# Relative-position rows of four heads in one product, stored once and repeated by a DMA within device memory

## The reference

```python
def _group_bias(rel_bias, g, dil):
    qi = np.arange(ATT_BLOCK)[:, None]            # ATT_BLOCK = 128
    kj = np.arange(2 * ATT_BLOCK)[None, :]
    dist = np.maximum(qi + ATT_BLOCK - kj, 0) * dil
    bucket = _t5_causal_bucket(dist)
    tab = rel_bias[:, g * ATT_HEADS_PER_GROUP:(g + 1) * ATT_HEADS_PER_GROUP]
    return jnp.transpose(tab[bucket], (2, 0, 1)).astype(jnp.float32)
...
    logits = jnp.einsum('zhnqd,zhnkd->zhnqk', qs, kb).astype(jnp.float32) * (hd ** -0.5)
    logits = jnp.where(valid, logits + bias[:, None], NEG_INF)
```

## Time and profile before

| | |
|---|---|
| median of 3 runs | 1987.79 us (1986.08, 1987.95, 1987.79) |
| the profiled execution | 1989.3 us; its span from first to last instruction 1987.5 us |
| PE busy | 1939.8 us, 98% of the span |
| DVE, ACT, POOL busy | 959.8, 779.9, 62.5 us |
| mean granted clock of PE | 0.989 of full |
| share of PE in the chain that ended last | 95% |

### The profile page before, as it was taken

How to read it: one execution, slowest core, us unless ns; L and a number is a source line. 1 busy time by engine, 2 the same in 40 slices (tenths; PEclk the granted TensorE clock), 3 DMA queues, 4 the chain that set the end, 5 groups by cost and what they waited for, 6 DMA issues and landing times.

```text
span 1987.5 us, 30907 instructions
## 1 busy us (share of the span) xinstructions
PE 1939.8 (98%) x12878; PEld 1607.1 (81%) x12878; DVE 959.8 (48%) x1515; ACT 779.9 (39%) x1221; POOL 62.5 (3%) x123
## 2 busy tenths in 40 slices
PE   7999988999999999999999999999999999999996
PEld 5887788868788888888699988788888888888885
DVE  6557634465444344446643226544344554344436
ACT  5354543362443133335543252332422442233343
POOL 0000000000320000000001100000000000000000
PEclk9999999999899999999999999999999999999998
DMA  4222100024432222222322222222233332222222
GB/s 168 97 82 78 64 24 4 14 64 138 128 114 96 96 97 102 98 96 95 106 86 86 86 75 97 84 75 78 82 120 117 108 100 96 96 96 95 96 85 85
DMA packets 51969, 178.99 MB, mean 90 GB/s; under 512 B 7103, under 2 KB 7615, under 8 KB 51840
## 3 DMA queue, kind: packets, MB, share of 16 engines
q1 hardware_dynamic: 45184, 161.50, 24.3%
q0 software_dynamic: 5968, 14.48, 2.4%
q10 hardware_dynamic: 688, 1.11, 0.2%
HBM read 168.41 MB, written 6.55 MB: 88 GB/s over the span
## 4 chain that ended last, share of the span: by engine, by line
PE 95%; DVE 2%; issue 1%; ACT 1%; DMA 0%; ACTq 0%; DVEq 0%
PE bank L659 94%; PE bank L841 0%; DVE ring_lo L1849 0%; PE bank L723 0%; DMA x<-in_xT 0%; DVE work_r L1905 0%; ACT work L1336 0%; PE bank L1266 0%; DVE nr L1863 0%; PE bank L813 0%; DVE hf L1885 0%; DVE work_r L1854 0%; DVE bias L2077 0%; DVE work L2297 0%; ACT ring_hi L1336 0%
## 5 line engine op out<-in xcount | busy, mean ns | idle before, releaser
L659 PE MATMUL bank<-work_r,ring_hi 128*128 128x512 f32 x2592 | 810.5, 392 | 14.5 <-DVE ring_lo L1849 13.2
L1849 DVE TENSOR_TENSOR ring_lo<-ring,ring_hi 128x1024 fp32r<-128x1024 f32 x302 | 367.8, 1224 | 626.1 <-ACT ring_hi L1336 626.0
L659 PEld LDWEIGHTS bank<-work_r,ring_hi 128*128 128x128 f32 x2592 | 488.2, 188 | 119.1 <-DVE ring_lo L1849 13.7
L1336 ACT ACTIVATE ring_hi<-ring 128x1024 fp32r<-128x1024 f32 x302 | 318.5, 1057 | 537.3 <-DMA ring<-in_stream 535.1
L659 PE MATMUL bank<-work_r,ring_lo 128*128 128x512 f32 x1296 | 506.8, 391 | 0.0
L659 PE MATMUL bank<-h_hi,ring_hi 128*128 128x512 f32 x864 | 341.5, 395 | 0.0
L659 PE MATMUL bank<-h_hi,ring_lo 128*128 128x512 f32 x864 | 337.7, 391 | 0.0
L659 PEld LDWEIGHTS bank<-work_r,ring_lo 128*128 128x128 f32 x1296 | 244.8, 189 | 50.8 <-issue 0.7
L659 PE MATMUL bank<-h_lo,ring_hi 128*128 128x512 f32 x864 | 212.3, 389 | 0.0
L659 PEld LDWEIGHTS bank<-h_hi,ring_hi 128*128 128x128 f32 x864 | 163.1, 189 | 40.7 <-issue 6.4
L659 PEld LDWEIGHTS bank<-h_hi,ring_lo 128*128 128x128 f32 x864 | 163.1, 189 | 34.7 <-issue 1.2
(11 more groups left out here) (226 smaller groups left out, 1590.1 us busy)
## 6 DMA issues: line engine op xcount, KB each, us to landing
ring<-in_stream SPq DMA_DIRECT2D x302, 512.0 KB, 3.3
scratch<-work POOLq DMA_DIRECT2D x12, 192.0 KB, 2.5
x<-in_xT POOLq DMA_DIRECT2D x8, 256.0 KB, 2.9
spill<-x POOLq DMA_DIRECT2D x1, 2048.0 KB, 9.2
work<-x POOLq DMA_DIRECT2D x32, 64.0 KB, 2.1
x<-spill POOLq DMA_DIRECT2D x8, 256.0 KB, 3.0
outT<-hf SPq DMA_DIRECT2D x8, 256.0 KB, 2.1
x<-in_xT ACTq DMA_DIRECT2D x2, 512.0 KB, 8.4
```

The costliest lines, as they stand in the source:

```text
L659: ins = pe.matmul(out, lhsT, rhs, start=start, stop=stop, skip_group_check=True)
L1336: return nc.scalar.activation(out, in_, func, **kw)
L1849: v.tensor_tensor(ring_lo[:, n % RING, :, :], ring[:, n % RING, :, :], ring_hi[:, n % RING, :, :], ALU.subtract).then_inc(sem("split_lo"), 1)
```

## The change

Three `rel` jobs take the place of 12: job g multiplies the whole table (33x12) by the constant matrix of group g, so that row c of its bank is head c's row. ACT copies 12 rows. POOL stores the four rows of the group once each, waits for the three stores, and then three DMAs within device memory copy each row 127 times (group 0) or 39 times (groups 1 and 2) behind it; POOL waits for them before the same 48 skewed reads. The waits of ACT on the stores go; DVE waits for the three row stores instead.

```diff
--- before.py
+++ after.py
@@ -234,7 +234,7 @@
     first = 1 if blk == 1 else 5
     j = [("wo", blk, m) for m in range(DT)]
     if blk == 1:
-        j += [("rel", c) for c in range(12)]
+        j += [("rel", g) for g in range(3)]
     for half in range(2):
         j += [("f1", blk, half, i) for i in range(FF_H)]
         if half == 0:
@@ -599,13 +599,17 @@
 
             pool.dma_start(g2_sb[0:16, :], wa2).then_inc(sem("wa2_in"), 16)
 
-            for c in range(12):
-                pool.wait_ge(*is_drained("rel", c))
-                pool.dma_start(scratch[c, 0:P * RELW].rearrange("(p n) -> p n", n=RELW),
-                               work[:, 40 + c % 4, 0:RELW]).then_inc(sem(f"rel_out{c % 4}"), 16)
+            for g in range(3):
+                pool.wait_ge(*is_drained("rel", g))
+                pool.dma_start(scratch[4 * g:4 * g + 4, 0:RELW], work[4 * g:4 * g + 4, 40 + g, 0:RELW]).then_inc(sem("rel_rows"), 16)
+            pool.wait_ge(sem("rel_rows"), 16 * 3)
+            for g in range(3):
+                copies = (P if g == 0 else 40) - 1
+                pool.dma_start(scratch[4 * g:4 * g + 4, RELW:RELW + copies * RELW].rearrange("c (p n) -> c p n", n=RELW),
+                               scratch[4 * g:4 * g + 4, 0:RELW].unsqueeze(1).broadcast_to([4, copies, RELW])).then_inc(sem("rel_out"), 16)
+            pool.wait_ge(sem("rel_out"), 16 * 3)
             for c in range(12):
                 g, hh = divmod(c, 4)
-                pool.wait_ge(sem(f"rel_out{c % 4}"), 16 * (c // 4 + 1))
                 skew = scratch[c, P - 1:P - 1 + P * (RELW - 1)].rearrange("(p n) -> p n", n=RELW - 1)
                 for z in range(TT):
                     r = slice(32 * z, 32 * z + 32)
@@ -1090,11 +1094,10 @@
                 project(("pb", m), plain(*ob) if m else arriving("ob_hi", "ob_lo", *ob), 4, 4)
                 done_with(1)
 
-            def rel(c):
-
-                out = take("rel", c)
-                single(("rel", c), [(out[:, 0:RELW], tab[0:33, c:c + 1].broadcast_to([33, P]),
-                                     work[0:33, 32 + c // 4, 0:RELW], True, True)])
+            def rel(g):
+
+                out = take("rel", g)
+                single(("rel", g), [(out[0:12, 0:RELW], tab[0:33, 0:12], work[0:33, 32 + g, 0:RELW], True, True)])
 
             def tail(blk):
                 n0 = 1 if blk == 1 else 5
@@ -1106,8 +1109,8 @@
                 if blk == 1:
                     pe.wait_ge(sem("relc_in"), 16)
                     pe.wait_ge(sem("tab_in"), 16)
-                    for c in range(12):
-                        rel(c)
+                    for g in range(3):
+                        rel(g)
                 for half in range(2):
                     if half == 0:
                         normed_together([("f1", blk, 0, i) for i in range(TOGETHER)], n0)
@@ -1608,12 +1611,10 @@
                 act.wait_ge(sem("merged1"), m + 1)
                 high_part(R(MERGED_HI + m), W(MERGED + m), "merged_hi1")
 
-            def copy_rel(c):
-                split_hi(blocks_to("rel", c))
-                act.wait_ge(*computed("rel", c))
-                if c >= 4:
-                    act.wait_ge(sem(f"rel_out{c % 4}"), 16 * (c // 4))
-                f(work[:, 40 + c % 4, 0:RELW], bank(("rel", c))[:, 0:RELW], ACT.Copy).then_inc(bank_drained[nth("rel", c)], 1)
+            def copy_rel(g):
+                split_hi(blocks_to("rel", g))
+                act.wait_ge(*computed("rel", g))
+                f(work[0:12, 40 + g, 0:RELW], bank(("rel", g))[0:12, 0:RELW], ACT.Copy).then_inc(bank_drained[nth("rel", g)], 1)
 
             def tail(blk):
                 n0 = 1 if blk == 1 else 5
@@ -1623,8 +1624,8 @@
                     high(n0, m)
                     square(n0, m)
                 if blk == 1:
-                    for c in range(12):
-                        copy_rel(c)
+                    for g in range(3):
+                        copy_rel(g)
 
                 act.wait_ge(sem(f"l{n0}"), DT)
                 act.wait_ge(sem("sq_added"), added(n0) + DT - 1)
@@ -1763,9 +1764,6 @@
             inverse_roots(lambda n: W(ROOT_G + n), [("gn", n) for n in range(4)], 256, 0, "root_g")
             gla_gates(2, 8)
 
-            for c in range(8, 12):
-                act.wait_ge(sem(f"rel_out{c % 4}"), 16 * (c // 4 + 1))
-
             def probs2(i, h, t):
                 near, far = reach(t)
                 n = near + 2 * far
@@ -2272,8 +2270,7 @@
                         scale_of(n0)
                     elif blk == 1:
 
-                        for c in range(4):
-                            dve.wait_ge(sem(f"rel_out{c}"), 48)
+                        dve.wait_ge(sem("rel_rows"), 16 * 3)
                     for m in range(DT):
                         split_lo(blocks_to("f2", blk, half, m))
                         dve.wait_ge(*computed("f2", blk, half, m))
```

## The result

The changed kernel takes 1977.24 us (median of 5 runs, 1975.02 to 1978.5), the kernel before 1987.61 us beside it (5 runs, 1985.49 to 1987.95). The ratio is 0.9946, with a 95% interval of 0.9935 to 0.9956: faster by 10.4 us, or 0.5%. The profiled execution is the one of 1977.24 us, with a span of 1975.4 us against 1987.5.

The account below looks back on a forecast made before the run. PE was taken as the bound, busy 1939.8 of 1987.5 us. Savings of 9.9 us (dropped products) and 2.4 us (clock in `f1`), all else zero, took 12.3 us off 1989.3: 1977.0 us, range 1974.0 to 1980.6.

Parts of the forecast that it names:

- Part 1: PE's `rel` stage: nine of 12 products go, so `f1` starts 2.2 us after `rel` starts; 9.9 us saved.
- Part 2: Start of `f1` on PE: the clock no longer falls to half, so the first twelve products save 2.4 us.
- Parts 3 and 4: Lost cover for `f1`'s inputs and weight ring, and ACT, POOL and DMA work: all off PE's path, zero.
- 4.5 us to spare: Weight ring: the fifth `f1` block would be ready at 541.6 and needed at 546.1.
- A wait on the ring: Sign of being wrong: PE waiting for weights (`ring_lo`), expected not to occur around the fourth to sixth `f1` job.
- The second rival: Copies on four engines take 13.7 us and make the fifth `f1` block 1.4 us late: 1978.4 us, chance 0.05.
- T - 12.3 us: PE's wait for the fifth `f1` block if its load queues behind all of a copy lasting T us.
- the fallen clock: Rival: the clock falls all the same, for 6.9 us in `f1`, losing 3.4 us: 1980.4 us, chance 0.13.
- The third rival: Copies at a third of the four-engine rate take 41 us, PE waits 28.7 us: 2005.7 us, chance 0.03.
- The sum: Whole kernel: 9.9 + 2.4 = 12.3 us off the profiled execution's 1989.3 us, giving 1977.0 us.
- the fall behind `z`: Half clock after the `z` stage, 6.9 us, might last half or twice as long: 1.7 us less or 3.4 more.

Follow-up runs that it names:

- the 12 thin products: The changed kernel with each of its three `rel` products made four times into the same bank: 1987.85 us against 1987.97 for the kernel before.
- the products over 128 rows: The kernel before with its 12 `rel` products made over all 128 rows, zeros in the table's 95 added rows: 1981.56 us against 1987.97.
- `z` over 128 rows: The turned copies plus the second block's four `z` products over 128 rows, 112 with zero weights: 1974.59 us against 1988.76 for the kernel before.
- The stores from SBUF: The changed kernel with 12 stores, each repeating one row 128 times from its SBUF partition, instead of device-memory copies: 2032.04 us against 1988.76 for the kernel before.
- the repeat: The changed kernel run again unaltered, in another set of runs: 1978.36 us against 1988.31 for the kernel before.
- turned copies: The changed kernel with the copies (128 or 48) as outermost dimension and the four heads inside: 1976.46 us against 1987.97 for the kernel before.
- later copies: The changed kernel with POOL waiting for the sixth `f1` job to be drained before issuing the copies: 1976.47 us against 1988.31 for the kernel before.

## Why the prediction was right

**Part 1** held: 2.03 us for the stage, 2.2 said; 10.1 saved, 9.9 said. That the output columns don't matter is shown by the 12 thin products.

**Part 2** held: no fall, 2.3 us against 2.4. Its reason, rows at work, was only read from two stages; the products over 128 rows and `z` over 128 rows show it.

**Parts 3 and 4** failed at one number, the time of the copies. I gave them 4.7 us, taken like stores from 128 partitions, and so the load of the fifth block 3.3 us, "4.5 us to spare". The copies take 13.6 us with no load beside them, and were in flight for 18.1 and 18.5 us in the two profiles; the load took 7.6 and 8.8. So the fifth block was late by 0.47 and 1.7 us, and the last skewed read was issued by 569.6 and not near 556. A wait on the ring stood among my signs of being wrong, and this one came true beside the right ones. It was too small to leave the range.

**The second rival** (few engines, a late fifth block, chance 0.05) had the copies right: 13.7 us said, 13.6 measured without loads. Its wait of 1.4 us lies near the measured ones, but partly by luck. It let the load wait for all of the copy, and its formula, T - 12.3 us, gives 5.8 us for T = 18.1. In fact the load was there at 543.0 and the copies ended at 546.1. (Part 2 calls the fallen clock the second rival; in the list it stands first.)

**The third rival** (slower copies) was right in kind and wrong in slope in the same way. With T = 30.7 the formula gives 18.4, and 8.4 was measured, since the load gets a part of the engines before the copies end. Against that, the clock falls in such a gap, which I had not counted. The stores from SBUF, 43 us slower, show how far a held-up weight load goes.

**The sum.** 12.3 us was said off the profiled execution; the stage, the start of `f1` and the new wait make 11.9 there. Between medians it is 10.4, and 10.0 in the repeat; without the wait, 11.5 (turned copies) and 11.8 (later copies). That 1977.0 came within 0.3 us of the measured 1977.24 is luck: it rests on a profiled execution 1.5 us above its median, and off the median the same sum gives 1975.5. My reason for keeping 1977.0, that this execution was slow because its clock fell early, isn't borne out: the products over 128 rows, which take the clock's cost away and nothing else, gain 6.4 us between medians, and the profiled execution had 6.6 to gain. That the fall behind `z` may be half as long was right, and is seen in three of the profiles.

## What to carry to other kernels

Where PE is the bound, look at the granted clock behind each stage of products with few rows at work: such a stage also slows what follows, and filling the idle rows with zero weights gave 6.4 us here, where dropping nine of 12 products gave 10.4. When work is moved from PE to a DMA, ask for how long it holds the DMA engines and where the ring of weights stands at that moment, and give a repeated copy its copies as the outermost dimension. A small float32 job costs its passages too, 0.44 us here.

## What was not expected of the hardware

Rows repeated 128 times, each out of one SBUF partition: 26 to 28 GB/s over all DMA engines at a busy share of about 0.9 and more, where with stores from 128 partitions the engines moved 268. Copies within device memory: 13.6 us for 1.26 MB with four as the outermost dimension, 18.1 beside weight loads, and 8.6 us for 1.38 MB with 128 or 48. And PE was busy all the time when its clock fell: 33 of 128 rows for 3.6 us did it, 33 rows for 2.0 us did not, nor did 33 rows for 4.0 us in the one execution profiled, and 128 rows for 7.9 us did not, though 95 of them had zero weights.
